# Second attention, seven of eight pairs: ScalarE makes a step's high parts ahead of the next step's probabilities

## The reference

```python
proj = x @ w_in
q, k, v, f_logit = split(proj)                        # 16 heads of 64
c = cumsum(log_sigmoid(f_logit + b_f), axis=1)        # a running sum per head
# for each block of 128 queries, over all keys up to it:
s = q_block @ k.T / sqrt(64) + c_q[:, None] - c_k[None, :]
s = where(key <= query, s, -inf)
pr = softmax(s)
o = pr @ v
mix = o @ w_out
```

## Time and profile before

| | |
|---|---|
| median of 3 runs | 2448.1 us (2447.31 to 2448.43) |
| the profiled execution's own time | 2446.86 us |
| its span, first to last instruction | 2445.1 us |
| PE busy | 2413.3 us, 99% of the span |
| DVE busy | 1569.6 us, 64% |
| ACT busy | 1099.1 us, 45% |
| POOL busy | 1370.4 us, 56% |
| mean granted TensorE clock | 0.999 of full |

### The profile page before, as it was taken

The page is one execution under the profiler, slowest core; times in us unless marked ns, Lnnn a source line. Parts: engine busy times, 40 slices in busy tenths (PEclk is TensorE's granted clock), DMA queues, the critical chain, the costliest instruction groups (busy, mean ns, idle before and its releaser), DMA issues. The chain is left out here.

```text
span 2445.1 us, 35804 instructions
## 1 busy us (share of the span) xinstructions
PE 2413.3 (99%) x11528; PEld 1995.9 (82%) x11528; DVE 1569.6 (64%) x2281; ACT 1099.1 (45%) x2030; POOL 1370.4 (56%) x1221
## 2 busy tenths in 40 slices
PE   8999999999999999999999999999999999999999
PEld 7788888888788878888888888877888888888887
DVE  8755552344777776445666666756868777777885
ACT  6433233301666661126777777832432333344441
POOL 5698887433455564343222222254289888666683
PEclk9999999999999999999999999999999999999999
DMA  4122223579210014332111111441133333487652
GB/s 144 61 82 64 69 72 112 181 273 324 87 34 26 26 35 168 134 120 71 61 61 60 60 60 57 150 131 52 56 112 125 112 119 112 146 277 220 189 183 83
DMA packets 128949, 275.65 MB, mean 113 GB/s; under 512 B 14144, under 2 KB 14528, under 8 KB 128848
## 3 DMA queue, kind: packets, MB, share of 16 engines
q1 hardware_dynamic: 84800, 157.85, 20.7%
q10 hardware_dynamic: 44048, 116.58, 13.3%
HBM read 206.41 MB, written 67.96 MB: 112 GB/s over the span
## 5 line engine op out<-in xcount | busy, mean ns | idle before, releaser
L686 POOL TENSOR_SCALAR whi<-raw 128x512 fp32r<-128x512 f32 x190 | 137.7, 725 | 332.7 <-PE bank L904 160.2
L688 POOL TENSOR_TENSOR wlo<-raw,whi 128x512 fp32r<-128x512 f32 x190 | 266.2, 1401 | 15.9
L701 POOL TENSOR_TENSOR wlo<-a,whi 128x512 fp32r<-128x512 f32 x114 | 165.0, 1448 | 46.9 <-ACT whi L1896 46.7
L904 PE MATMUL bank<-b_lo,whi 128*128 128x512 f32 x448 | 175.1, 391 | 0.0
L904 PE MATMUL bank<-a_hi,whi 128*128 128x512 f32 x400 | 158.6, 397 | 3.5 <-DVE a_lo L2805 2.3
L967 PE MATMUL bank<-b_hi,whi 128*128 128x512 f32 x384 | 157.0, 409 | 0.2 <-ACT f_raw L1682 0.2
L967 PE MATMUL bank<-b_hi,wlo 128*128 128x512 f32 x384 | 150.7, 392 | 0.0
L967 PE MATMUL bank<-b_lo,whi 128*128 128x512 f32 x384 | 150.0, 391 | 0.0
L812 POOL COPY fc<-fc 128x128 f32<-128x128 f32 x96 | 28.1, 292 | 193.2 <-DVE mx L2735 193.2
L1896 ACT ACTIVATE whi<-a 128x512 fp32r<-128x512 f32 x114 | 70.6, 627 | 134.3 <-PE bank L1247 51.6
L904 PE MATMUL bank<-b_hi,whi 128*128 128x512 f32 x320 | 125.3, 392 | 1.0 <-ACT up_g L2290 0.6
(11 more groups left out here) (793 smaller groups left out, 7870.2 us busy)
## 6 DMA issues: line engine op xcount, KB each, us to landing
raw<-in_w SPq DMA_DIRECT2D x202, 256.0 KB, 2.6
a<-in_pairs SPq DMA_DIRECT2D x152, 256.0 KB, 2.7
fc<-c_scr ACTq DMA_DIRECT2D x32, 512.0 KB, 3.6
wd_scr<-wd SPq DMA_DIRECT2D x55, 256.0 KB, 5.3
wd<-in_down SPq DMA_DIRECT2D x44, 256.0 KB, 4.8
xs_scr<-made ACTq DMA_DIRECT2D x40, 256.0 KB, 2.7
h_scr<-up_y ACTq DMA_DIRECT2D x13, 512.0 KB, 2.6
raw<-wd_scr SPq DMA_DIRECT2D x26, 256.0 KB, 2.9
```

Source lines behind the costliest of these rows:

```text
L686: nc.gpsimd.tensor_scalar(hi, src, 1.0, 1.0, ALU.mult, ALU.mult).then_inc(w_hi, 1)
L688: nc.gpsimd.tensor_tensor(lo, src, hi.bitcast(F32), ALU.subtract).then_inc(w_lo, 1)
L701: nc.gpsimd.tensor_tensor(ring[1][pos], src[:].rearrange("p (k c) -> p k c", c=P), ring[0][pos].bitcast(F32), ALU.subtract).then_inc(ww_lo, 1)
L904: last = nc.tensor.matmul(psum_ap, ws[w][:, k, :], a[:, kt, hs(h)], start=(first and i == 0 and j == 0), stop=(final and i == n - 1 and j ...
```

## The change

In the seven pairs with a following pair, and in their steps 0 to 13, ScalarE does `high` for the chunks of step s first and `normalise(s + 1)` behind them. In step 13 of the seventh pair that is still ahead of two loads that the same engine issues. Step 14 had this order already, and step 15 has nothing to normalise behind it. In the last pair the condition is written out anew and gives the order that it had. No instruction is added or taken away, and no other engine's list changes.

```diff
                     if not fills and s:
                         ple_out(s - 1)
-                    if s + 1 < NST and s != NST - 2 and (fills or s > 0):
+                    if not fills and 0 < s < NST - 2:
                         normalise(s + 1)
                     for n in CHUNKS_OF[s]:
                         high(n)
+                    if fills and s < NST - 2:
+                        normalise(s + 1)
                     if s == NST - 3 and isinstance(it, int) and it * 2 + pp == NPAIR - 2:
                         p_load(0)
                         p_load(1)
```

## The result

| | before | after |
|---|---|---|
| median of 6 runs | 2448.26 us (2447.04 to 2448.91) | 2461.07 us (2459.04 to 2461.23) |
| span of the profiled execution | 2445.1 us | 2459.4 us |
| PE busy | 2413.3 us | 2416.2 us |
| ACT busy | 1099.1 us | 1092.6 us |

The ratio is 1.0051, with a 95% interval of 1.0041 to 1.006. The forecast was 2461.7.

A forecast was written before the change was run, and what follows sets the result against it. TensorE, busy for 99% of the span, was taken to bound the kernel. Delays of 1.25 + 0.69 = 1.94 us a pair, 13.6 us over seven pairs, led to a forecast of 2461.7 us, range 2452.5 to 2469.

The forecast's parts named there:

- the term of step 7: Transposes of step 7 wait for `normalise` of step 7, now behind `high` of step 6; 0.68 us a pair by itself.
- Steps 3 to 6: `normalise` of step 4 delays `expo` of step 5 by 0.73; transposes of steps 5 and 6 start 0.34 and 0.57 late.
- Steps 6 to 7: `high` of step 6 waits for `values`, `normalise` comes last; TensorE is 1.25 us late at the transposes of step 7.
- too short to cover: TensorE's own 1.47 us between `values` and the transposes of step 7 cannot hide about 2.1 us on ScalarE.
- Steps 7 to 11: Steps 8 to 11 have narrow rows or four parts of fill; nothing counted.
- Steps 12 to 14: `normalise` of step 13 delays `expo` of step 14 by 0.84; transposes of step 14 start 0.69 us late.
- rival 2: No difference: TensorE's own stretch covers the later probabilities and step 3's lateness is taken up; 2448 us, chance 0.07.
- ScalarE's idle time before `high`: Predicted sign in the profile: this wait, ended by `values`, grows by about 1 us a pair at step 6.
- The later load of running sums: Load behind `expo` in steps 4, 5, 12, 13 goes out up to 0.84 us later; counted at nothing.
- A gain from earlier high parts: Faster rival: earlier `high` brings earlier low parts, removing TensorE's 3.4 us of waits before transposes; 2444 us, chance 0.04.
- The clock stayed at 1.00: Answers the clock rival: new gaps trigger one fall to 1.2 GHz per pair, 24 us more, 2485 us; chance 0.03.

The follow-up runs named there:

- Step 3 alone: Kernel before with the new order only in step 3 of the seven pairs; 2452.57 us, ratio 1.0019.
- taken out alone: The full change with only step 6 put back to the old order; 2455.88 us in one run.
- the kernel with step 6 alone: Kernel before with the new order only in step 6 of the seven pairs; 2452.34 us, ratio 1.0019.
- the test with moved fill: The full change with one part of TensorE's fill moved from step 7 to step 6; 2461.12 us, ratio 1.0053.
- 0, 1, 2 and 7 to 11: Kernel before with the new order only in steps 0, 1, 2 and 7 to 11; 2449.75 us, ratio 1.0008.
- Step 2 costs 0.32 alone: Kernel before with the new order only in step 2; 2448.12 us in one run.

## Why the prediction was right, step by step

**The sum.** 13.6 us forecast, 12.8 between the medians and 13.5 in the seven pairs of the profiled executions; a pair 1.94 forecast, 1.93 measured. That the pair agrees to 0.01 us is in part luck: the term of step 7 came out 0.12 larger, and 0.08 that the sum did not have was regained behind it (both below).

**Steps 3 to 6.** 0.34 and 0.57 late at steps 5 and 6 were forecast; 0.36 and 0.58 came. Step 3 alone gives the first of them exactly, which shows that the start is `expo` of step 5 behind `normalise` of step 4.

**Steps 6 to 7.** The increment was forecast at 0.68 and is 0.80 in the change, 0.72 alone, and 0.73 of pair length when taken out alone. About half of the 0.12 in the change is the latency from the end of `normalise` to the first transpose, which I took as 0.06 us; here it is 0.13 in the third pair of the change and in that of the kernel with step 6 alone. The other half is that `high` of step 6 starts 0.64 late from the start of the pair and not 0.57, as the `values` ahead of it do. The place and the releaser are as forecast. My words that TensorE's own work is "too short to cover" hold for the transposes of step 7, but the test with moved fill shows that work taken there from step 7 does not help: the chain behind them is full too. Whether work from a later step would was not tried.

**Steps 7 to 11** I counted at nothing behind the transposes of step 7, and nothing is added there; but 0.08 us is regained, which I had not seen. Between the transposes of steps 8 and 9 the lateness falls from 1.37 to 1.29 in the change, and by 0.07 or 0.08 in the three other kernels with the old amount of fill and the new order in step 7 (0.36 to 0.28 with 0, 1, 2 and 7 to 11). In those with the old order in step 7 (2, 3 or 6 alone) it does not fall. Before, the `values` of step 7 waited for its low part, which ends at 1271.00 + 0.68 = 1271.68; the transpose ahead of them starts at 1271.66:

```profile
1269.78 0.58 ACT L1747 ACTIVATE fp_hi<-flip 128x512 fp32r<-128x512 f32 x1
...
1271.00 0.68 DVE L2749 TENSOR_TENSOR fp_lo<-bank,fp_hi 128x512 fp32r<-128x512 f32 x1
...
1271.74 0.39 PE L1160 MATMUL pv<-fp_hi,fv 128*128 128x256 f32 x1
```

After, where the transpose ahead starts at 1277.25:

```profile
1275.27 0.60 ACT L1747 ACTIVATE fp_hi<-flip 128x512 fp32r<-128x512 f32 x1 [0.44 <-PE flip L1145]
...
1276.51 0.68 DVE L2751 TENSOR_TENSOR fp_lo<-bank,fp_hi 128x512 fp32r<-128x512 f32 x1
...
1277.28 0.36 PE L1160 MATMUL pv<-fp_hi,fv 128*128 128x256 f32 x1
```

`high` no longer stands behind the `normalise` of step 8, so it starts 0.68 behind the first transpose of step 7 instead of 0.79, the low part 1.92 instead of 2.01, and the `values` 0.03 behind the transpose ahead instead of 0.08. That is 0.05 of the 0.08; for the rest the rows name no wait.

**Steps 12 to 14.** 0.69 forecast, 0.67 measured between steps 13 and 14.

**What was wrong though the sum was right.** At step 1, too, the transposes before start late (0.43 us behind the product ahead instead of 0.23), where I wrote that at all but those of step 6 everything lies ready. I named steps 3, 5 and 13 as covered in rival 2, and left steps 0 to 2 out without a word of their wait. Step 2 costs 0.32 alone, and step 13 about 0.55. In the full change neither shows, since step 3 delays the same `expo` of step 5 by more than step 2 does (0.72 us alone against 0.34), and step 12 delays the low part of step 13 by more than `normalise` needs (in the change that low part ends at 1298.46, and `normalise` of step 14 at 1297.03 + 1.05 = 1298.08). These costs don't add; the latest arrival decides. The terms alone, 0.73 + 0.66 + 0.80 + 0.32 and some 0.55, would make 3.1 us a pair where the change has 1.93.

**The waits and the load.** I said that ScalarE's idle time before `high` would grow by about 1 us a pair at step 6. There it is 1.36 us in the third pair, and over all steps it grew by 4.4 a pair (9.5 to 40.3 us in seven). The later load of running sums cost nothing that shows: no wait of `maxima` for it stands among VectorE's waits, before or after.

**The rivals.** A gain from earlier high parts came only in step 7, 0.08 us a pair; before the transposes that wait, the low parts start later, not earlier, and ScalarE's saved wait for reciprocals (18 us in all) bought nothing more. The clock stayed at 1.00 in all seven pairs, with gaps of up to 0.8 us on TensorE. The rule of the Trainium skill (TensorE: Matmul & The Clock Gate, section "A second HAM failure mode: psum-queue depth-cycling"), by which frequent short idles between groups of matmuls can make the clock swing, does not show here.

## What to carry to other kernels

In an in-order list, keep what is ready early ahead of what waits: a piece of work that fits into the wait of its neighbour is free there; put behind the neighbour, it can cost most of its length downstream (here 0.66 us a pair for a piece of 1.15, and 0.80 for one of 0.94), or nothing, where what follows has the slack. Follow each moved start through every wait of the instructions behind it, the ones that come only on even steps too, and take the latest arrival at each place instead of adding the terms. Before filling a gap on the bounding engine, see whether the chain behind it has room; in the one case tried here it had none, and the time was lost again one group later.

## What the runs showed that I had not expected

That a start of 0.5 us at step 2 passes four steps and three engines and reaches TensorE at step 6 as 0.35; and that from the recorded end of ScalarE's instruction to the first dependent transpose it took 0.13 or 0.14 us in the third pair of three kernels, where from VectorE's it takes 0.06. It is not a matter of the engine alone: in the seventh pair of the same three kernels ScalarE's took 0.05, and VectorE's there took 0.15 in the change, as in the kernel before. Why these differ was not tried.
